# Turning x of the state-space part by DMA instead of on TensorE, in a two-block transformer kernel on one core

## The chip, the cores and the metric

The kernel runs on 1 core of one Trainium2 chip. The metric is the device time of one execution in microseconds (us), lower is better. The engines are PE (TensorE), DVE (VectorE), ACT (ScalarE), POOL (GpSimd) and SP (SyncE, which here only issues DMAs).

## The reference, cut to what matters

Two blocks of two layers each, on 256 tokens of width 1024, in float32. The change lies in the first block, in each of its two layers. There the input projection gives z, x, B, C, dt, q, k, v and gates. x, B and C go through a causal convolution of 4 taps and a silu; then x (2048 channels, 32 heads in 4 groups) runs through a chunked state-space scan:

```python
xbc = jax.nn.silu(causal_depthwise_conv(xbc, conv_w, conv_b)).astype(f32)
xs, bm, cm = jnp.split(xbc, [SSD_INNER, SSD_INNER + SSD_GROUPS * SSD_STATE], axis=-1)
x = (xh * dt[..., None]).reshape(bsz, nc, SSD_CHUNK, SSD_GROUPS, SSD_HPG, p)
y_diag = jnp.einsum("bgecls,bcsgep->bclgep", cb[:, :, None] * decay, x)
states = jnp.einsum("bclgn,bclgep->bcgepn", bc, x * decay_states[..., None])
y = ssd_chunked(xs, dt, a, bm, cm) + d_skip.astype(f32)[:, None] * xs
y = y.reshape(bsz, s, SSD_INNER) * jax.nn.silu(z.astype(f32))
yg = yg * lax.rsqrt(jnp.mean(yg * yg, axis=-1, keepdims=True) + RMS_EPS)
return (yg.reshape(bsz, s, SSD_INNER) * norm_w.astype(f32)).astype(z.dtype)
```

Beside it the layer has an attention with three query patterns over 8 heads (queries and keys are turned so that head channels lie on the partitions), and after it output projections and a gated feed-forward.

## The kernel before, in words

**The weight stream.** All large products run as three TensorE products on float32 values split in two: high times high, high times low, low times high. The weights come in chunks of 128 x 2048 (one `load` on SP into a ring of 3 slots, `w_raw`). ACT copies a chunk to `w_high` (`split_high`, L1180), DVE subtracts to `w_low` (`split_low`), PE multiplies (L676 to L678 with the tokens stationary, 24 products a chunk of 512 columns; L937 to L939, for x, B and C, with the weights stationary, 48 of 256). ACT's split of chunk c waits until PE has finished chunk c-3, SP's load of chunk c until DVE has split chunk c-3. Each engine's program is one loop over chunks c, and the small work is put between chunks by hand: "at c" below means in that engine's iteration c. ACT and DVE therefore reach their iteration c while PE is about at chunk c-2, and SP reaches its own while PE is about at c-5. Two chunks make a tile of 512 projected columns; x tiles are i = 2, 5, 8, 11 (`XT`), one for each group g.

**The state-space work of group g, before.** ACT convolves a part and takes the silu into `conv` at c = 2i+6. PE turns the eight 128 x 128 blocks of `conv` at c = 2i+5 into PSUM banks 4 and 5 (`turn`, L681; from group 1 on it first waits for `ssd_y`, the last sum of the group before, made by DVE). DVE reads the banks at c = 2i+7: `y` = x times d_skip, `xdt` = x times dt (two token tiles each), `xds`. PE at c = 2i+6 and 2i+8 spreads the rows of decays (L789, from `DR`, a small DMA `decay_rows`), at 2i+7 makes the new state from `xds` (L795), at 2i+9 and 2i+10 multiplies `xdt` by the masked decays `EM` (L802) and applies the state (L807). ACT takes exponentials of the spread rows (L1346), DVE masks them (L1949 and the next product).

**The small DMAs of SP.** The decay rows of group 0 are both loaded at SP's c = 13, those of the others at 2i+6 and 2i+8. Before the change SP issues at each c first the weight load, then a turn of q or k, then a turn of y, then one of attention weights, then decay rows.

**Turning by DMA.** y of each group, and seven of the eight query and key tiles, are turned by transfers: POOL lays the 16-bit halves of the float32 words apart (L1669 for y, L1662 for q and k), SP issues a transpose of 16-bit elements (L592, L581), and POOL (y, L1672) or ACT (q and k, L1325) puts the halves together. y then gets its norm weights on DVE, ACT copies it to `b_high`, DVE subtracts to `b_low`, all at c = 2i+16 (`Y_WEIGH`). POOL's program is one fixed order: for n = 0 to 3 the halves of q or k tile n, then those of y group n and their putting together.

**The last query tile** (`q5`) is turned by PE at c = 47 (`QK_LAST`) into banks 6 and 7. Bank 7 holds the output of attention head 3 until DVE has made its `b_low`, so PE waits for `o_ready` 4.

Of the kernel before, what the change touches and what calls it, by code (L numbers as in the profile page):

```python
# [143 lines left out]
def build(nc, stream, pars, const1, const2, onehot, relb, final_g, ple_g, w_x, out, rev):  # L144
    ctx = ExitStack()
    with ctx:
# [63 lines left out]
        def words(name, at_col, shape):  # L210
# [40 lines left out]
        y_back = [words("y_turned0", Q_AT + 1024, [2 * T * 512])[:, :], words("y_turned1", Q_AT + 1024, [2 * T * 512])[:, :],  # L251
                  early("y_turned2", 0, 20, 2 * T * 512, U16)[:, :], early("y_turned3", 0, 20, 2 * T * 512, U16)[:, :]]
        pT = E0[:, 1152:1536]
# [118 lines left out]
        xt_ps = signal("xt_ps", GROUPS)  # L372
# [5 lines left out]
        words_split = signal("words_split", 7 + GROUPS)  # L378
        words_turned = [signal("words_turned0", 16 * 6), signal("words_turned1", 16 * 5)]
# [34 lines left out]
        y_high = signal("y_high", 2 * GROUPS)  # L414
# [27 lines left out]
        xdt_ready = signal("xdt_ready", GROUPS)  # L442
# [3 lines left out]
        y_weighted = signal("y_weighted", 2 * GROUPS)  # L446
# [12 lines left out]
        xds_ready = signal("xds_ready", GROUPS)  # L459
# [100 lines left out]
        def _(sp):  # L560
# [14 lines left out]
            def turn_qk(l, c):  # L575

                for n, at_c in enumerate(QK_SPLIT):
                    m = QK_TURN[n]
                    if c == at_c + 3:
                        sp.wait_ge(words_split.sem, words_split.at(l, m + 1))  # L580
                        sp.dma_start_transpose(qk_turn[n].rearrange("p (m r) -> p m r", r=P), qk_half[n])\  # L581
                            .then_inc(words_turned[m % 2].sem, 16)

            def turn_y(l, c):

                for g, i in enumerate(XT):
                    m = Y_TURN[g]
                    if c == 2 * i + 16:
                        if g == 2:
                            sp.wait_ge(xt_ps.sem, xt_ps.at(l, GROUPS))  # L590
                        sp.wait_ge(words_split.sem, words_split.at(l, m + 1))
                        sp.dma_start_transpose(y_back[g].rearrange("p (m r) -> p m r", r=P), y_half[g])\  # L592
                            .then_inc(words_turned[m % 2].sem, 16)
# [80 lines left out]
        def _(pe):  # L674
# [42 lines left out]
            def before(l, c):  # L717
# [1684 lines left out]
```

## Time and profile before

| | |
|---|---|
| median of 3 runs | 1533.62 us (1533.17 to 1533.92) |
| the profiled execution: its time | 1532.54 us |
| its span (first to last instruction) | 1530.7 us |
| granted TensorE clock, mean | 0.999 |
| busy: PE, PE weight loads | 1510.8 us (99%), 1277.3 us (83%) |
| busy: DVE, ACT, POOL | 1043.2 us (68%), 919.3 us (60%), 178.5 us (12%) |
| DMA engines, mean busy share of the hardware queue | 58.3% |

The profile is of one execution. A busy time is the time in which an engine worked on an instruction; matmuls are pipelined, so that the distance from one start to the next tells what one costs, not its own length. The time of the profiled execution is 1.84 us above its span.

### The profile page before, as it was taken

How to read it: one execution, taken by the hardware profiler on the slowest of the kernel's cores; microseconds unless marked ns; L12 is line 12 of the kernel's file. 1: busy time of each engine (PE TensorE's matmuls, PEld its weight loads, DVE VectorE, ACT ScalarE, POOL GpSimd, SP SyncE). 2: the span in 40 equal slices, each digit the busy share in tenths (PEclk: the TensorE clock that was granted, in tenths of full speed). 3: DMA queues.
4: the chain of work that ended last, by engine and by line, in shares of the span. 5: the costliest groups of instructions: out<-in, count | busy, mean ns of one | idle time of the engine just before them, and what ended most of it. 6: DMA issues, size and time to landing. Idle time of an engine off the chain costs nothing.

```text
span 1530.7 us, 18991 instructions
## 1 busy us (share of the span) xinstructions
PE 1510.8 (99%) x7628; PEld 1277.3 (83%) x7628; DVE 1043.2 (68%) x1324; ACT 919.3 (60%) x1100; POOL 178.5 (12%) x113
## 2 busy tenths in 40 slices
PE   7999999999999999999999999999999999999998
PEld 7888888878888888988888888888888878888887
DVE  6978887856665555787887775666555576677665
ACT  5766786564355553667678565436555465666564
POOL 1001121412000100001112231100010020002000
PEclk9999999999999999999999999999999999999999
DMA  7456655766457775455556695547768574447541
GB/s 276 166 174 169 193 170 197 203 191 164 181 189 212 211 229 181 169 165 182 175 180 192 186 220 165 172 146 240 210 168 261 196 258 180 145 145 245 177 152 66
DMA packets 128239, 287.03 MB, mean 188 GB/s; under 512 B 92919, under 2 KB 93848, under 8 KB 97688
## 3 DMA queue, kind: packets, MB, share of 16 engines
q1 hardware_dynamic: 127048, 283.39, 58.3%
q10 hardware_dynamic: 1104, 2.43, 0.5%
q8 instruction: 60, 0.98, 0.2%
q14 instruction: 27, 0.22, 0.0%
HBM read 261.69 MB, written 1.84 MB: 172 GB/s over the span
## 4 chain that ended last, share of the span: by engine, by line
PE 86%; DVE 9%; ACT 3%; issue 1%; DMA 0%; ACTq 0%; DVEq 0%
PE ps L676 23%; PE ps L678 23%; PE ps L677 23%; DVE w_low L1706 3%; PE ps L681 3%; DVE conv L1792 2%; PE ps L937 2%; PE ps L939 2%; PE ps L938 2%; PE ps L824 1%; DVE scratch L1706 1%; ACT w_high L1180 1%; PE ps L802 1%; PE ps L826 1%; DVE xpad L1706 1%
## 5 line engine op out<-in xcount | busy, mean ns | idle before, releaser
L1706 DVE TENSOR_TENSOR w_low<-w_raw,w_high 128x2048 fp32r<-128x2048 f32 (+1 forms) x250 | 575.0, 2300 | 374.2 <-ACT w_high L1180 307.3
L676 PE MATMUL ps<-w_high,u_high 128*128 128x512 f32 x1376 | 547.8, 398 | 0.5 <-DVE w_low L1706 0.5
L678 PE MATMUL ps<-w_high,u_low 128*128 128x512 f32 x1376 | 537.0, 390 | 0.0
L677 PE MATMUL ps<-w_low,u_high 128*128 128x512 f32 x1376 | 536.2, 390 | 0.0
L1180 ACT ACTIVATE w_high<-w_raw 128x2048 fp32r<-128x2048 f32 (+1 forms) x196 | 369.1, 1883 | 250.5 <-PE ps L678 237.5
L676 PEld LDWEIGHTS ps<-w_high,u_high 128*128 128x128 f32 x1376 | 258.6, 188 | 55.2 <-issue 2.4
L678 PEld LDWEIGHTS ps<-w_high,u_low 128*128 128x128 f32 x1376 | 258.3, 188 | 55.1
L677 PEld LDWEIGHTS ps<-w_low,u_high 128*128 128x128 f32 x1376 | 258.8, 188 | 53.7 <-issue 2.4
L676 PE MATMUL ps<-w_high,b_high 128*128 128x512 f32 x384 | 151.6, 395 | 0.0
L678 PE MATMUL ps<-w_high,b_low 128*128 128x512 f32 x384 | 149.8, 390 | 0.0
L677 PE MATMUL ps<-w_low,b_high 128*128 128x512 f32 x384 | 149.6, 389 | 0.0
L1430 ACT ACTIVATE w_high<-w_raw 128x2048 fp32r<-128x2048 f32 x50 | 95.3, 1911 | 45.8 <-PE ps L678 45.6
L937 PE MATMUL ps<-u_high,w_high 128*128 128x256 f32 x384 | 112.8, 294 | 4.0 <-DVE w_low L1706 3.7
L938 PE MATMUL ps<-u_low,w_high 128*128 128x256 f32 x384 | 109.2, 284 | 0.0
L939 PE MATMUL ps<-u_high,w_low 128*128 128x256 f32 x384 | 109.2, 284 | 0.0
L1706 DVE TENSOR_TENSOR scratch<-scratch 128x128 f32<-128x128 f32 (+3 forms) x156 | 68.1, 470 | 34.5 <-ACT scratch L1373 27.1
L678 PEld LDWEIGHTS ps<-w_high,b_low 128*128 128x128 f32 x384 | 72.1, 188 | 15.2
L677 PEld LDWEIGHTS ps<-w_low,b_high 128*128 128x128 f32 x384 | 72.2, 188 | 14.5
L676 PEld LDWEIGHTS ps<-w_high,b_high 128*128 128x128 f32 x384 | 72.2, 188 | 14.2
L937 PEld LDWEIGHTS ps<-u_high,w_high 128*128 128x128 f32 x384 | 74.2, 193 | 6.5 <-DVE w_low L1706 4.1
L938 PEld LDWEIGHTS ps<-u_low,w_high 128*128 128x128 f32 x384 | 74.3, 194 | 1.7 <-issue 1.4
L939 PEld LDWEIGHTS ps<-u_high,w_low 128*128 128x128 f32 x384 | 74.2, 193 | 0.0
(242 smaller groups left out, 1512.3 us busy)
## 6 DMA issues: line engine op xcount, KB each, us to landing
w_raw<-in_stream SPq DMA_DIRECT2D x238, 1024.0 KB, 4.9
w_raw<-in_stream SPq DMA_DIRECT2D x12, 512.0 KB, 4.1
par<-in_pars SPq DMA_DIRECT2D x4, 269.0 KB, 5.7
h<-in_x SPq DMA_DIRECT2D x4, 256.0 KB, 4.9
ple_gain<-in_ple_g ACTq DMA_DIRECT2D x2, 512.0 KB, 4.8
out<-h SPq DMA_DIRECT2D x4, 256.0 KB, 2.0
scratch<-in_const SPq DMA_DIRECT2D x1, 768.0 KB, 7.3
rev<-scratch ACTq DMA_DIRECT2D x1, 768.0 KB, 3.6
```

Source lines behind the costliest of these rows:

```text
L676: nc.tensor.matmul(o, hi, whi, start=start, stop=False, **kw)
L677: nc.tensor.matmul(o, hi, wlo, start=False, stop=False, **kw)
L678: return nc.tensor.matmul(o, lo, whi, start=False, stop=stop, **kw)
L681: return nc.tensor.transpose(o, i, ident)
L802: last = nc.tensor.matmul(ps[:, 4 + t, e * HD:(e + 1) * HD], EM[t][:, e, :], xdt[:, t, e * HD:(e + 1) * HD], start=True, stop=True)
L937: nc.tensor.matmul(o, WH[:, slot, w], uH[:, kk, :], start=first, stop=False, skip_group_check=True)
L938: nc.tensor.matmul(o, WH[:, slot, w], uL[:, kk, :], start=False, stop=False, skip_group_check=True)
L939: last = nc.tensor.matmul(o, WL[:, slot, w], uH[:, kk, :], start=False, stop=kk == KD - 1, skip_group_check=True)
L1180: nc.scalar.activation(WH[:, c % RING, 0:n], W[:, c % RING, 0:n], ACT.Copy).then_inc(high_ready, 1)
L1430: nc.scalar.activation(WH[:, n % RING, :], W[:, n % RING, :], ACT.Copy).then_inc(high_ready, 1)
L1706: return nc.vector.tensor_tensor(out=o, in0=a, in1=b, op=op)
L1792: ins = nc.vector.scalar_tensor_tensor(out=conv[:, j, :], in0=xpad[:, j, k:k + S], scalar=par[:, w:w + 1], in1=conv[:, j, :], op0=ALU.mult ...
```

## The change

It does these things, in each of the two layers:

1. PE no longer turns `conv`. POOL lays the halves of `conv` apart (`split_x`, two copies), SP issues a transpose (`turn_x`, at c = 2i+9, ahead of all its other small DMAs of that c) into `x_turned`, which lies where `conv` lies, and POOL puts them together in `xdt` (`merge_x`).
2. DVE works from `xdt` at c = 2i+8 instead of from PSUM at 2i+7: y, `xds`, and then `xdt` times dt in place.
3. PE makes the new state at c = 2i+8, behind the decay rows of token tile 1, in bank 5; ACT copies it at 2i+10.
4. POOL's order becomes: x of group g, y of group g-1 (halves and putting together), then the halves of q or k tile g. y's transposes move from c = 2i+16 to 2i+17. The semaphores of the transfers go from two to three.
5. y's weighting is folded: ACT makes `b_high` by four scaled copies, DVE makes `b_low` by four fused multiply-subtracts (`Y_HIGH`, `Y_LOW`).
6. The last query tile is turned into banks 4 and 5, without the wait for `o_ready` 4. ACT's putting together of tile q2 moves from c = 30 to 31.

```diff
-        QK_TURN, Y_TURN = (0, 2, 4, 6, 8, 9, 10), (1, 3, 5, 7)
-        QK_MERGE = (14, 24, 30, 34, 46, 47, 48)
+        X_TURN, QK_TURN, Y_TURN = (0, 2, 5, 8), (1, 4, 7, 10, 12, 13, 14), (3, 6, 9, 11)
+        QK_MERGE = (14, 24, 31, 34, 46, 47, 48)
-        Y_WEIGH = 16
+        X_AT = 8
+        Y_HIGH, Y_LOW = (17, 17, 17, 16), (19, 19, 19, 16)
...
+            def turn_x(l, c):
+                for g, i in enumerate(XT):
+                    m = X_TURN[g]
+                    if c == 2 * i + 9:
+                        sp.wait_ge(words_split.sem, words_split.at(l, m + 1))
+                        sp.dma_start_transpose(x_back.rearrange("p (m r) -> p m r", r=P),
+                                               x_half.rearrange("p h t j n -> p (h t j n)")).then_inc(words_turned[m % 3].sem, 16)
...
-                    if c == 2 * i + 16:
+                    if c == 2 * i + 17:
...
+                    turn_x(l, c)
                     turn_qk(l, c)
                     turn_y(l, c)
...
-                    if c == 2 * i + 5:
-                        pe.wait_ge(conv_act.sem, conv_act.at(l, 3 + g))
-                        if g == 0:
-                            pe.wait_ge(btok_out.sem, btok_out.at(l, 1))
-                            pe.wait_ge(cumt_out.sem, cumt_out.at(l, 1))
-                        else:
-                            pe.wait_ge(ssd_y.sem, ssd_y.at(l, 2 * g))
-                        for t in range(T):
-                            for j in range(4):
-                                last = turn(ps[:, 4 + t, tok(j)], conv[:, j, tok(t)])
-                        last.then_inc(xt_ps.sem, 1)
...
-                    if c == 2 * i + 7:
-                        pe.wait_ge(xds_ready.sem, xds_ready.at(l, g + 1))
+                    if c == 2 * i + 8:
+                        pe.wait_ge(x_ready.sem, x_ready.at(l, 2 * g + 1))
...
-                        nc.tensor.matmul(ps[:, 6, :], btok[:, g, :], xds, start=True, stop=True).then_inc(state_ps.sem, 1)
+                        nc.tensor.matmul(ps[:, 5, :], btok[:, g, :], xds, start=True, stop=True).then_inc(state_ps.sem, 1)
...
                 if c == QK_LAST:
                     pe.wait_ge(roped.sem, roped.at(l, 8))
-                    pe.wait_ge(o_ready.sem, o_ready.at(l, 4))
...
+                        if c == 2 * i + Y_HIGH[g]:
+                            act.wait_ge(y_whole.sem, y_whole.at(l, g + 1))
+                            for j in range(4):
+                                jj = 4 * g + j
+                                ins = nc.scalar.activation(bH[:, jj, :].rearrange("p (t n) -> p t n", t=T), Y[g % 2][:, :, tok(j)],
+                                                           ACT.Identity, scale=par[:, C_SN + jj:C_SN + jj + 1])
...
+                def split_x(g):
+                    pool.wait_ge(conv_act.sem, conv_act.at(l, 3 + g))
+                    for t in range(T):
+                        ins = nc.gpsimd.tensor_copy(x_half[:, :, t], conv[:, :, tok(t)].bitcast(U16).rearrange("p j (n h) -> p h j n", h=2))
+                    ins.then_inc(words_split.sem, 1)
+
+                def merge_x(g):
+                    m = X_TURN[g]
+                    pool.wait_ge(words_turned[m % 3].sem, words_turned[m % 3].at(l, 16 * (m // 3 + 1)))
+                    if g:
+                        pool.wait_ge(yd_ps.sem, yd_ps.at(l, 2 * g))
+                    nc.gpsimd.tensor_copy(words_of(xdt).rearrange("p n h -> p h n"),
+                                          x_back.rearrange("p (h m) -> p h m", h=2)).then_inc(x_whole.sem, 1)
...
+                for g in range(GROUPS):
+                    split_x(g)
+                    if g == 0:
+                        split_qk(0)
+                    merge_x(g)
+                    if g:
+                        split_y(g - 1)
+                        merge_y(g - 1)
+                        split_qk(g)
+                split_y(3)
+                merge_y(3)
...
+                        if c == 2 * i + X_AT:
+                            dve.wait_ge(x_whole.sem, x_whole.at(l, g + 1))
...
+                            for t in range(T):
+                                tt(heads(y[:, t, :]), heads(xdt[:, t, :]),
+                                   bc(par[:, C_DS + g * HPG:C_DS + (g + 1) * HPG].unsqueeze(2), HPG, HD), ALU.mult)
+                            tt(heads(xds), heads(xdt[:, 0, :]), bc(dt_out[:, g * HPG:(g + 1) * HPG].unsqueeze(2), HPG, HD), ALU.mult)\
+                                .then_inc(x_ready.sem, 1)
```

## Rows read from the trace of the kernel before

**Rows 1.** The page's head and its busy time of PE.

```profile
span 1530.7 us, 18991 instructions
PE 1510.8 (99%) x7628; PEld 1277.3 (83%) x7628; DVE 1043.2 (68%) x1324; ACT 919.3 (60%) x1100; POOL 178.5 (12%) x113
```

**Rows 2.** Who waited for whom: us in total, times, longest us.

```profile
ACT w_high L1180 <- PE ps L678: 237.5, 109, 4.5
...
PE ps L681 <- DVE b_low L1706: 3.4, 2, 1.7
```

**Rows 3.** Instructions on `conv`, and what ended the idle time before them.

```profile
L681 PE MATMUL ps<-con,conv x64: 270/273/301, 70.6 to 793.6; 128*128 128x128 f32 x64
...
  DVE scratch L1706: 1.6, 4
```

**Rows 4.** PE's timeline in group 0: start us, us, engine, line, what.

```profile
70.27 0.39 PE L678 MATMUL ps<-w_high,u_low 128*128 128x512 f32 x1
70.59 1.06 PE L681 MATMUL ps<-con,conv 128*128 128x128 f32 x8
...
71.72 0.39 PE L677 MATMUL ps<-w_low,u_high 128*128 128x512 f32 x1
...
76.96 0.63 PE L789 MATMUL ps<-decay_rows,steps_r 128*128 128x512 f32 x2
...
89.78 0.63 PE L789 MATMUL ps<-decay_rows,steps_r 128*128 128x512 f32 x2
```

**Rows 5.** PE's timeline where the last query tile is turned.

```profile
319.89 0.39 PE L678 MATMUL ps<-w_high,u_low 128*128 128x512 f32 x1
321.98 1.06 PE L681 MATMUL ps<-con,scratch 128*128 128x128 f32 x8 [1.71 <-DVE b_low L1706]
```

**Rows 6.** ACT's timeline: the silu of x, group 0.

```profile
67.62 1.06 ACT L1272 ACTIVATE conv<-conv 128x1024 f32<-128x1024 f32 x1 [3.39 <-DVE conv L1792]
```

**Rows 7.** DVE's timeline: two stretches of group 0, one later.

```profile
67.50 2.29 DVE L1706 TENSOR_TENSOR w_low<-w_raw,w_high 128x2048 fp32r<-128x2048 f32 x1
...
83.91 1.21 DVE L1706 TENSOR_TENSOR ssd_decay<-ssd_decay,scratch 128x1016 f32<-128x1016 f32 x1
...
246.32 3.95 DVE L1706 TENSOR_TENSOR w_low<-w_raw,w_high 128x2048 fp32r<-128x2048 f32 x1 [2.87 <-ACT w_high L1180]
```

**Rows 8.** POOL's timeline: laying halves apart, and putting y together.

```profile
79.75 1.89 POOL L1662 COPY qk_halves<-scratch 128x2048 uint16<-128x2048 uint16 x1 [49.52 <-DVE scratch L1706]
...
245.67 2.51 POOL L1672 COPY scratch<-y_turned 128x2048 uint16<-128x2048 uint16 x1 [4.36 <-DMA y_turned<-y_halves]
```

**Rows 9.** POOL's groups by form: count, then busy us and mean ns.

```profile
L1682 POOL COPY act_halves<-scratch 128x1024 uint16<-128x1024 uint16 x22 | 22.9, 1041 | 338.3 <-DVE scratch L1706 338.3
```

**Rows 10.** SP's timeline of issues: start us, us that SP was held.

```profile
69.81 0.33 SPq L606 DMA_DIRECT2D w_raw<-in_stream  x1
70.26 1.53 SPq L573 DMA_DIRECT2D decay_rows<-cum_rows  x2
...
84.32 5.28 SPq L581 DMA_TRANSPOSE qk_turned<-qk_halves  x1
...
119.23 3.16 SPq L592 DMA_TRANSPOSE y_turned<-y_halves  x1
```

**Rows 11.** DMA issues: count, KB each where told, median us from issue to landing.

```profile
w_raw<-in_stream SPq DMA_DIRECT2D x238, 1024.0 KB, 4.9
...
qk_turned<-qk_halves SPq DMA_TRANSPOSE x14, 7.4
...
y_turned<-y_halves SPq DMA_TRANSPOSE x8, 4.3
```

**Rows 12.** DVE's groups by form: count, then busy us and mean ns.

```profile
L1792 DVE SCALAR_TENSOR_TENSOR conv<-xpad,par,conv 128x256 f32<-128x256 f32 x144 | 60.1, 480 | 0.9
...
L1706 DVE TENSOR_TENSOR scratch<-ps,par 128x512 f32<-128x512 f32 x32 | 21.7, 684 | 7.9 <-PE ps L681 7.9
...
L1706 DVE TENSOR_TENSOR scratch<-scratch,par 128x512 f32<-128x512 f32 x16 | 13.7, 895 | 0.0
```

More of the change, by code:

```diff
@@ L377, in build @@
         qk_ps = signal("qk_ps", 1)
-        words_split = signal("words_split", 7 + GROUPS)
-        words_turned = [signal("words_turned0", 16 * 6), signal("words_turned1", 16 * 5)]
+        words_split = signal("words_split", 7 + 2 * GROUPS)
+        words_turned = [signal(f"words_turned{i}", 16 * 5) for i in range(3)]
+        x_whole = signal("x_whole", GROUPS)
         y_whole = signal("y_whole", GROUPS)
@@ L809, in before @@
                     pe.wait_ge(roped.sem, roped.at(l, 8))
-                    pe.wait_ge(o_ready.sem, o_ready.at(l, 4))
                     for hh in range(4):
                         for t in range(T):
-                            last = turn(ps[:, 6 + hh // 2, (hh % 2) * S + t * P:(hh % 2) * S + (t + 1) * P], ev[QK[7][2]][:, t, tok(hh)])
+                            last = turn(ps[:, 4 + hh // 2, (hh % 2) * S + t * P:(hh % 2) * S + (t + 1) * P], ev[QK[7][2]][:, t, tok(hh)])
                     last.then_inc(qk_ps.sem, 1)
@@ L1348, in _ @@
                                 ins.then_inc(ssd_exp.sem, 1)
+                        if c == 2 * i + 10:
+                            act.wait_ge(state_ps.sem, state_ps.at(l, g + 1))
+                            if g:
+                                act.wait_ge(off_ps.sem, off_ps.at(l, g))
+                            nc.scalar.activation(state, ps[:, 5, :], ACT.Copy).then_inc(state_out.sem, 1)
                         if c == 2 * i + 13:
@@ L1359, in _ @@
                             nc.scalar.activation(gsum, gsum, ACT.Sqrt, bias=eps1, scale=GROUPS / INNER).then_inc(group_root.sem, 1)
-                        if c == 2 * i + Y_WEIGH:
-                            for t in range(T):
-                                act.wait_ge(y_weighted.sem, y_weighted.at(l, 2 * g + t + 1))
-                                nc.scalar.activation(bH[:, 4 * g:4 * g + 4, tok(t)], four(Y[g % 2][:, t, :]), ACT.Copy)\
-                                    .then_inc(y_high.sem, 1)
+                        if c == 2 * i + Y_HIGH[g]:
[4 more added lines that the diff above has]
+                                                           ACT.Identity, scale=par[:, C_SN + jj:C_SN + jj + 1])
+                            ins.then_inc(y_high.sem, 1)
                     for n in range(8):
@@ L1951, in _ @@
                                     .then_inc(ssd_m.sem, 1)
+                        if c == 2 * i + X_AT:
+                            dve.wait_ge(x_whole.sem, x_whole.at(l, g + 1))
+                            if g >= 2:
+                                dve.wait_ge(y_ready.sem, y_ready.at(l, 2 * g - 2))
+                            if g:
+                                dve.wait_ge(state_ps.sem, state_ps.at(l, g))
+                            else:
+                                dve.wait_ge(decays.sem, decays.at(l, 1))
+                                chain.then(dve, tt(dt_out, dt[:, 0:HEADS], dec_out, ALU.mult))
+                            for t in range(T):
[3 more added lines that the diff above has]
+                                .then_inc(x_ready.sem, 1)
+                            for t in range(T):
+                                ins = tt(heads(xdt[:, t, :]), heads(xdt[:, t, :]),
+                                         bc(dt[:, t * HEADS + g * HPG:t * HEADS + (g + 1) * HPG].unsqueeze(2), HPG, HD), ALU.mult)
+                            ins.then_inc(x_ready.sem, 1)
                         if c == 2 * i + 12:
@@ L1973, in _ @@
                             convolve(l, n, c - 2 * i - CONV_AT)
+                    for g, i in enumerate(XT):
+                        if c == 2 * i + Y_LOW[g]:
+                            dve.wait_ge(y_high.sem, y_high.at(l, g + 1))
+                            for j in range(4):
+                                jj = 4 * g + j
+                                ins = nc.vector.scalar_tensor_tensor(
+                                    out=bL[:, jj, :].rearrange("p (t n) -> p t n", t=T), in0=Y[g % 2][:, :, tok(j)],
+                                    scalar=par[:, C_SN + jj:C_SN + jj + 1],
+                                    in1=bH[:, jj, :].bitcast(F32).rearrange("p (t n) -> p t n", t=T), op0=ALU.mult, op1=ALU.subtract)
+                            ins.then_inc(y_ready.sem, 2)
                     for n, (name, i, e, _) in enumerate(QK):
```

113 lines of the change are left out of this document (48 added, 65 removed).

## The prediction

> **What bounds the kernel now.** I read the page's head first: PE is busy 99% of the span [rows 1]. On this page that alone doesn't say that PE is the bound, since overlapping matmuls count as busy, so I looked at who waits for whom. ACT, which prepares the weights, stands idle for 237.5 us until PE has freed a slot, and PE's largest wait for another engine inside a layer is one of 3.4 us in two pieces [rows 2]. So the weight stream runs ahead of PE, and PE's own instruction stream sets the time. What a change is worth is then what it takes out of PE's stream, less every wait that it puts in. The reader should look at PE's timeline around one insert: products, eight small ones, products again without a pause [rows 4].
>
> **The sum is made for the profiled execution**, 1532.54 us (span 1530.7 and 1.84 around it). The median of the runs shown is 1533.62, so 1.08 is added at the end.
>
> **What leaves PE.** (a) The turns of conv, 64 matmuls in 8 blocks [rows 3]. In group 0 the last product before the block starts at 70.27, the second one after it at 71.72, 1.45 us later. From 71.72 to the next insert at 76.96 there are 23 steps, 0.228 us each [rows 4]. Two steps would have taken 0.46, so a block costs 0.99 us and eight cost 7.9. (b) PE's waits for ssd_y right before these blocks, 1.6 us in 4 places [rows 3]. The insert that asks for ssd_y next comes one chunk later (some 5.5 us, the distance of 24 steps), far more than the 0.4 of each wait, so they don't come back. (c) The last query tile: the product before it starts at 319.89, the turn at 321.98, and the wait for b_low of head 3 is named there with 1.71 [rows 5], in total 3.4 for both layers [rows 2]. Banks 4 and 5 are free by then, because the scores of head 3 were read before the rope of that tile, in DVE's order. What is late next is the scores of head 4, which wait for ACT's copy of the turned tile; ACT makes it behind the split of chunk 49, and PE has a whole chunk of products before it asks. I take 3.4. Sum of what leaves: 12.9 us.
>
> **What moves on PE** is the state product. It now follows directly on the spreading of decays, an insert that is there anyway. The number of instructions is the same. I cost it at nothing, from -0.2 to +0.2 a group.
>
> **What comes in: the decay rows of group 0.** SP issues both of them at c = 13, and turn_x of group 0 is at c = 13 too and stands ahead. This is the one place where a new transfer is on PE's path. Step by step, on the clock of the trace of before:
> - The silu of x ends at 67.62 + 1.06 = 68.68 [rows 6]. POOL then makes two copies of 1024 words each; the same size costs 1.04 [rows 9]. DVE has begun a w_low at 67.50 that takes 2.29 [rows 7], and if POOL must wait for it, the copies run from 69.79 to 71.87; if not, they end at 70.8.
> - SP has issued its weight load at 69.81 and then issued the rows from 70.26 at once [rows 10]. Now it waits until 71.87, and the transpose holds it: 3.16 us for y's with nothing ahead, 5.28 for a q or k one behind a weight load [rows 10]. So SP comes free between 75.0 and 77.1, and the rows of token tile 0 need half of 1.53 more.
> - A transpose lands 4.3 us after its issue (y, mostly alone) or 7.4 (q and k, behind a load) [rows 11]: at 76.2 or at 79.3. The weight load ahead of it is 2.1 us old of its 4.9 [rows 11], so 2.8 us of it are left, which the 3.16 that SP needs in any case mostly cover. I take 1.3 us above the lower end: 77.5 for transpose and rows behind it.
> - PE comes to L789 at 76.96 - 0.99 = 75.97 [rows 4]. It waits 1.5 us. The bounds are 0 (rows land as soon as they are issued, 75.8) and 3.3 (behind a transpose that takes 7.4).
>
> Two layers: 3.0 us, from 0 to 6.6. No other group has this, since their rows are issued at 2i+6 and 2i+8 and turn_x at 2i+9.
>
> The Trainium skill (DMA: Bandwidth & Descriptors, section on queues, rings and completion order) says that a DMA engine takes the descriptors of a ring in order and that a completion is only written after the engine's earlier writes. By it the rows can't be reported before the transpose, so the wait is at least 76.2 - 75.97 = 0.2 us; no row of this trace shows a small transfer behind a transpose.
>
> **The rest, costed at nothing, with its cover.** Chain of x in group 0: POOL does the halves of k0 before merge_x. Even where they stand now, at 79.75 for 1.89, the merge (2.51, as y's [rows 8]) would end at 84.2; DVE wants xdt when its mask of the decays ends, 83.91 + 1.21 = 85.1 [rows 7]. Three products follow (0.68 each [rows 12]), and PE asks for xds behind L789 at 89.78 + 0.5 [rows 4]: 87.1 against 90.3, some 3 us of cover, less about 1 in later groups, where PE has gained on it. The weight loads behind a transpose on SP start up to 5.3 us late (ring of three, one chunk of 5.5 us each). DVE gets lighter: y loses two products of 0.895 and two subtracts, and gets four fused ones of 0.48 [rows 12]. ACT gets four scaled copies for two plain ones, under 1 us a group, against 237.5 us of waiting for PE [rows 2].
>
> **Result of the sum:** 12.9 - 3.0 = 9.9 us; 1522.6 for the profiled execution, 1523.7 for the median.
>
> **Rivals.**
> - A, the rows come in time (POOL's copies don't wait for DVE and the small transfer is quick): nothing is paid, 12.9 us gained, 1520.7. For it: 70.8 + 3.16 + 0.8 = 74.8, before 75.97. Against it: the load in front. 0.16.
> - B, slower: DVE and POOL hold each other. A w_low that began 0.65 us after POOL's merge of y took 3.95 instead of 2.29, and would have begun its work when that merge ended at 248.18 [rows 7, 8]. Per group three new POOL copies come, and they fall where DVE splits chunk 2i+8 and works on x. If the merge of x and the halves of y hold it back to back, 2.51 + 1.89 = 4.4 us, the 2 to 3 us of cover are gone and PE waits for xds some 2.2 us in each of 8 groups: 17.6 - 9.9 = 7.7 us slower, 1541.3. It decides from 1.2 us of wait a group on. Against it: merge_x waits for its transfer, and by the numbers above the merge of group 0 is over before DVE's mask is. 0.08. The Trainium skill (SBUF — State Buffer, section on the two separate sides) says that a DVE instruction with two inputs in SBUF and a GpSimd one exclude each other for their whole length, and an input in PSUM is no part of this. The trace agrees with the first (3.95); by the rule the products on x, which read PSUM before and don't now, join those that can be held.
> - C, the last group's y: its transpose moves one c on and behind a weight load (7.4 in place of 4.3), while its b_high stays at c = 38, ahead of the exponentials and weight splits on ACT. If PE then waits in the first attention heads, up to 2.5 us a layer, 5 of the 9.9 go: 1528.7. For it: it is the only y stage without its extra chunk. Against it: two chunks of stream lie ahead. 0.13.
> - D, nothing is gained (within 0.2%): the stream of weights falls back by as much as PE gains, and PE waits for w_low. Against it stands the 237.5 us [rows 2]. 0.06.
>
> **Chances and range.** The likeliest case, the sum with its rows of group 0 late, 0.57; its own range is 1520.7 to 1527.3 (0 to 6.6 us paid). A measurement of this kernel tells 0.2%, 3.07 us, from no change. Faster by more: 0.57 + 0.16 + 0.13 = 0.86. Same: D, 0.06. Slower: B, 0.08. The range reaches from A with a little more at the turned query tile (1.86 by the starts of rows 5 in place of 1.71), 1520.0, over C to 1529.5; B and D stay outside.
>
> **What would show it.** PE has no L681 on conv and no wait for b_low or ssd_y. A new wait of 1 to 2 us at L789, once a layer, ended by a DMA of decay_rows. SP's timeline has a DMA_TRANSPOSE of 3 to 5.3 us right before the two rows of group 0. If PE waits at L795 for a DVE product, B is at work; if it waits at L824 or for w_low about chunks 38 to 42, C or D. The prediction is wrong if the rows of group 0 wait much over 3.3 us, or if waits for x appear in all groups.

## The result, and the profile after

The changed kernel takes 1545.51 us (1544.63 to 1548.32) beside 1533.53 for the kernel before on the same chip: a ratio of 1.0082, 95% interval [1.0068, 1.0096]. It is 0.8% slower. The prediction of 1523.7 (1520.0 to 1529.5), with 0.86 for faster, was wrong. The profiled execution took 1545.49 us.

The page's head, beside [rows 1]:

```profile
span 1543.2 us, 18921 instructions
...
PE 1511.1 (98%) x7564; PEld 1275.6 (83%) x7564; DVE 1064.4 (69%) x1324; ACT 924.0 (60%) x1116; POOL 254.8 (17%) x137
```

PE has 64 instructions fewer, as meant, yet is as busy as before (1511.1 against 1510.8), although the prediction had put the turns at 7.9 us. And the span is 12.5 us longer. So two things need finding: time in which PE waits, and time in which it works slower.

What PE waits for (total, times, longest), beside [rows 2]:

```profile
PE ps L799 <- DVE scratch L1749: 14.2, 4, 5.0
...
PE ps L789 <- DMA decay_rows<-cum_rows: 2.8, 2, 1.4
```

The waits for `b_low` (3.4) and `ssd_y` (1.6) are gone. In their place stands L799, the state product, which waits for DVE's `xds` in 4 places: in groups 2 and 3 of each layer. PE's timeline in group 2 of the first layer:

```profile
168.90 0.63 PE L789 MATMUL ps<-decay_rows,steps_r 128*128 128x512 f32 x2
172.53 1.13 PE L799 MATMUL ps<-scratch 128*128 128x512 f32 x2 [2.99 <-DVE scratch L1749]
```

What DVE did in these microseconds (its timeline; compare [rows 7]):

```profile
159.77 1.66 DVE L2014 SCALAR_TENSOR_TENSOR b_low<-scratch,par,b_high 128x256 fp32r<-128x256 f32 x4
164.06 3.71 DVE L1749 TENSOR_TENSOR w_low<-w_raw,w_high 128x2048 fp32r<-128x2048 f32 x1 [2.62 <-ACT w_high L1186]
167.69 1.86 DVE L1975 COPY ssd_decay<-scratch 128x8 f32<-128x8 f32 x1
169.46 1.21 DVE L1749 TENSOR_TENSOR ssd_decay<-ssd_decay,scratch 128x1016 f32<-128x1016 f32 x1
170.59 1.28 DVE L1749 TENSOR_TENSOR scratch<-xdt,par 128x512 f32<-128x512 f32 x2
171.79 0.68 DVE L1749 TENSOR_TENSOR scratch<-xdt,small 128x512 f32<-128x512 f32 x1
```

and POOL's timeline beside it:

```profile
163.12 2.56 POOL L1670 COPY xdt<-x_turned 128x2048 uint16<-128x2048 uint16 x1 [10.65 <-DMA x_turned<-x_halves]
165.60 3.92 POOL L1678 COPY y_halves<-scratch 128x2048 uint16<-128x2048 uint16 x1
```

Read them together. DVE's `w_low` starts at 164.06, while POOL's merge of x runs until 165.68, and takes 3.71 where one alone takes 2.29 [rows 7]. POOL's next copy, the halves of y, starts at 165.60 and is itself held by `w_low`; when `w_low` ends at 167.77, the halves hold DVE's next instruction, a copy of 128 x 8 elements, until 169.52. It takes 1.86. DVE lost 1.42 + 1.69 = 3.1 us, and PE's gap is 2.99. DVE never waits for `x_whole`: the transfer of x is in time, but it is in time at the wrong moment.

The same two instructions are held for 2.6, 2.6 and 3.0 us in the other three places (`w_low` takes 3.16, 3.16 and 3.63 there, the small copy 1.86 each time), 11.3 us in all, beside 14.2 us of waits.

Why the merge stands there is seen on SP's timeline (start, time that SP was held; compare [rows 10]):

```profile
154.64 0.34 SPq L616 DMA_DIRECT2D w_raw<-in_stream  x1
155.03 5.48 SPq L591 DMA_TRANSPOSE x_turned<-x_halves  x1
```

POOL has the halves of x ready at 152.47. SP issues a weight load at 154.64 first, and the transpose behind it holds SP for 5.48 us and lands at 163.07.

The slower work shows when stretches are asked for (columns: us, then busy us and count of PE, PEld, DVE, ACT, POOL; then the granted clock, DMA share, GB/s):

```profile
217.00:221.80 4.80, 4.80 (x10) 3.09 (x11) 4.77 (x10) 4.09 (x5) 2.66 (x1) 0.50 0.55 108
778.30:781.60 3.30, 3.30 (x9) 2.61 (x8) 3.30 (x8) 1.10 (x2) 2.00 (x1) 0.50 0.25 55
822.70:826.00 3.30, 3.30 (x9) 2.20 (x8) 3.30 (x6) 3.21 (x5) 1.55 (x1) 0.50 0.41 92
1242.50:1245.80 3.30, 3.30 (x9) 2.61 (x8) 0.62 (x1) 3.30 (x5) 0.00 (x0) 0.50 0.91 313
222.00:228.00 6.00, 6.00 (x36) 5.26 (x35) 6.00 (x5) 2.10 (x2) 5.35 (x2) 1.00 0.54 198
```

In four stretches the granted clock is 0.50, that is 1.2 in place of 2.4 GHz. The starts of the stream's products lie 0.43 us apart there, where [rows 4] give 0.228:

```profile
1239.11 2.84 PE L1046 MATMUL ps<-scratch 33*128 33x384 f32 x8
...
1243.29 0.63 PE L688 MATMUL ps<-w_low,u_high 128*128 128x512 f32 x1
1243.72 0.63 PE L689 MATMUL ps<-w_high,u_low 128*128 128x512 f32 x1
```

The stretches run from 215.04 to 221.87 (PE stands until 216.80 of it), and over 3.41 us each from 778.24, 822.61 and 1242.45. PE works 5.07 + 3 x 3.41 = 15.3 us in them; at half speed that is 7.6 us lost, an estimate (with 0.228 in place of 0.43 a step it would be 7.1). Before, only the tail after 1528.9 was at that clock. The first three begin during or right behind PE's waits at L799 of 4.98, 2.41 and 3.83 us; ahead of the fourth PE has no gap over 0.3 us, but the block of eight small products shown above (33 rows each, 1239.11 to 1241.95).

The balance: 12.9 us leave by the prediction's sum, 2.8 + 14.2 + 7.6 = 24.6 come, 11.7 more in all; the spans of the two profiled executions differ by 12.5 and their times by 12.95.

The place of group 0 that the prediction had priced, PE's timeline and SP's:

```profile
75.87 0.39 PE L689 MATMUL ps<-w_high,u_low 128*128 128x512 f32 x1
77.64 0.71 PE L789 MATMUL ps<-decay_rows,steps_r 128*128 128x512 f32 x2 [1.39 <-DMA decay_rows<-cum_rows]
```

```profile
71.84 3.42 SPq L591 DMA_TRANSPOSE x_turned<-x_halves  x1
75.39 1.53 SPq L574 DMA_DIRECT2D decay_rows<-cum_rows  x2
```

### The profile page after: what moved, and what is told of

Its sections match the earlier page's. It is cut to its first block, busy times and chain, and to the rows that moved or that the text cites. A ratio compares the mean times of both kernels' runs of the same rounds, so it can differ in the third digit from the quotient of the medians.

```text
span 1543.2 us, 18921 instructions
## 1 busy us (share of the span) xinstructions
PE 1511.1 (98%) x7564; PEld 1275.6 (83%) x7564; DVE 1064.4 (69%) x1324; ACT 924.0 (60%) x1116; POOL 254.8 (17%) x137
## 4 chain that ended last, share of the span: by engine, by line
PE 79%; DVE 13%; ACT 4%; issue 3%; DMA 0%; SPq 0%; POOL 0%; ACTq 0%; DVEq 0%
PE ps L687 22%; PE ps L689 22%; PE ps L688 22%; DVE w_low L1749 4%; DVE conv L1835 3%; DVE scratch L1749 2%; PE ps L692 2%; PE ps L943 2%; PE ps L944 1%; PE ps L945 1%; PE ps L830 1%; ACT w_high L1186 1%; PE ps L808 1%; DVE ssd_decay L1975 1%; ACT ssd_decay L1349 1%
## 5 line engine op out<-in xcount | busy, mean ns | idle before, releaser
L1749 DVE TENSOR_TENSOR scratch<-scratch 128x128 f32<-128x128 f32 (+3 forms) x156 | 83.3, 566 | 34.6 <-ACT scratch L1383 27.2
L689 PEld LDWEIGHTS ps<-w_high,b_low 128*128 128x128 f32 x384 | 72.1, 188 | 15.3
L1725 POOL COPY act_halves<-scratch 128x1024 uint16<-128x1024 uint16 x22 | 22.9, 1043 | 340.1 <-DVE scratch L1749 340.1
```

The source lines that it names most:

```text
L689: return nc.tensor.matmul(o, lo, whi, start=False, stop=stop, **kw)
L1725: nc.gpsimd.tensor_copy(act_half[j % 2][:, :].rearrange("p (h n) -> p h n", h=2), ac_words[j % 2].rearrange("p n h -> p h n")).then_inc(ac ...
L1749: return nc.vector.tensor_tensor(out=o, in0=a, in1=b, op=op)
```

## The experiments

The theories. **Hold** (rival B of the prediction): DVE and POOL exclude each other; the merge of x and the halves of y fall on DVE's `w_low` and small copy and make `xds` late. **Place**: PE now asks for `xds` at a point where DVE can't have it, whatever holds it, since two products of y and the mask stand ahead in DVE's order. **Cascade**: wherever the state product stands, the lateness comes back at the next thing that depends on it. The kernel before ran beside each, with medians of 1533.1 to 1533.6; ratios are against it.

### 1. POOL: halves of y ahead of the merge of x

```diff
-                    merge_x(g)
                     if g:
                         split_y(g - 1)
+                    merge_x(g)
+                    if g:
                         merge_y(g - 1)
```

> The changed kernel with POOL's order altered in one place: the halves of y of group g-1 are laid apart before x of group g is put together, not after it. All copies and all waits for data stay. Theory hold (DVE and POOL exclude each other, and two POOL copies back to back hold DVE's w_low and then the small copy ahead of the mask, so xds comes late): POOL then does y's halves while x is still under way, only one copy falls on chunk 2i+8, the small copy isn't held for 1.7 us, and PE's waits for xds fall from 14.2 us to 5 or less, TensorE's clock stays at its upper level in most places, 1531 to 1536. Theory place (PE asks for the state one chunk too early, whatever POOL does): the waits stay over 10 us, 1541 to 1546.

Measured: 1532.68 us, ratio 1.0000 [0.9991, 1.0009]; 12.8 us less than the changed kernel, from swapping two copies of POOL. L799 waits 6.8 us in place of 14.2 (hold had said 5 or less), no stretch before the tail is at the lower clock, and PE is busy 1503.8 us, 7.3 less. DVE's timeline at the same place, and POOL's:

```profile
164.63 3.52 DVE L1750 TENSOR_TENSOR w_low<-w_raw,w_high 128x2048 fp32r<-128x2048 f32 x1 [0.98 <-ACT w_high L1186]
168.07 0.16 DVE L1976 COPY ssd_decay<-scratch 128x8 f32<-128x8 f32 x1
```

```profile
160.50 2.08 POOL L1678 COPY y_halves<-scratch 128x2048 uint16<-128x2048 uint16 x1 [7.44 <-DVE scratch L2005]
163.46 2.59 POOL L1670 COPY xdt<-x_turned 128x2048 uint16<-128x2048 uint16 x1 [0.88 <-DMA x_turned<-x_halves]
```

The small copy is back at 0.16, since the halves of y are over before `w_low` starts; `w_low` is still held by the merge (3.52). Place is refuted as the main cause: PE asks where it asked, DVE's order is what it was. It isn't excluded for a part of the 6.8 us that are left.

### 2. The state product a chunk later

PE's product first, ACT's copy of the state second:

```diff
-                    if c == 2 * i + 8:
+                    if c == 2 * i + 9:
-                        if c == 2 * i + 10:
+                        if c == 2 * i + 11:
```

> The changed kernel with PE's state product at 2i+9 and ACT's copy of it at 2i+11, one chunk later each; POOL and DVE unaltered. Hold and place both expect that the waits for xds go (14.2 us) and with them the time that PE spent at the lower clock behind them (some 7 us): 1523 to 1526. A third theory, cascade (DVE has fallen behind the weight stream, and what isn't waited for here is waited for at the next w_low or decay product), expects new waits at the products with decays or at w_low and 1533 or more.

Measured: 1545.41 us, 1.0080 [1.0065, 1.0095]: nothing gained, where hold and place had said 1523 to 1526. L799 has no wait any more, but another has come up:

```profile
PE ps L808 <- ACT scratch L1356: 11.4, 4, 3.4
```

PE's product with the state waits for ACT's copy of it. On ACT that copy stands behind the convolution of the next part, which waited 5.25 us for DVE's `xpad`, and `b_high`:

```profile
185.83 2.08 ACT L1272 ACTIVATE conv<-xpad,par 128x256 f32<-128x256 f32 x4 [5.25 <-DVE xpad L1749]
187.81 1.69 ACT L1372 ACTIVATE b_high<-scratch,par 128x256 fp32r<-128x256 f32 x4
189.41 0.57 ACT L1356 ACTIVATE scratch<-ps 128x512 f32<-128x512 f32 x1
```

Giving PE's instruction a chunk more time gave the wait to the next one. And the lower clock stayed: four stretches behind or at these waits, in which PE works 19.1 us, about 9.5 us lost by the same estimate (7.6 in the changed kernel). Cascade holds for this edit.

### 3. The kernel before with the last query tile in banks 4 and 5

```diff
-                    pe.wait_ge(o_ready.sem, o_ready.at(l, 4))
-                            last = turn(ps[:, 6 + hh // 2, ...
+                            last = turn(ps[:, 4 + hh // 2, ...
```

> The kernel before with one part of the change alone: the last query tile is turned into banks 4 and 5 without the wait for head 3's low part. The prediction's step says 3.4 us less than before (3.7 by the starts of the products): 1530.0 +- 0.3, the wait for b_low gone. The rival for this step is that the wait turns up again at the scores of head 4, then 1533.5.

Measured: 1529.57 us, 0.9975 [0.9965, 0.9984]: 0.25% of 1533 is 3.8 us, against a term of 3.4, a little more than was expected. The wait for `b_low` is gone and nothing took its place.

### 4. The products on x ahead of the second mask

DVE's block of products on x at 2i+8 is moved as a whole ahead of its mask of the decays at the same c.

> The changed kernel with DVE's products on x ahead of the mask of the decays within chunk 2i+8; POOL and PE unaltered. Hold: the small copy that was held for 1.7 us and the mask of 1.2 us no longer stand ahead of xds, which comes some 3 us earlier, so PE's waits of 3.0, 5.0, 2.4 and 3.8 us shrink to about 0, 2, 0 and 1: 1529 to 1534. Place: DVE is simply too full between the split of 2i+8 and PE's question, the mask comes late in its stead and PE waits at the product with decays, 1540 or more.

Measured: 1543.81 us, 1.0071 [1.0054, 1.0088]. L799 waits 12.4 us in 4 places. This missed what the hold theory said (1529 to 1534), and the time is what place had said (1540 or more), but not for place's reason: no wait came up at the products with decays. The holds moved: in group 2 `w_low` began first and POOL's merge of x was held to 4.13 us; DVE waited 2.44 us for it, and then the halves of y held the two products of y, which took 2.92 us in place of 1.28. Reordering DVE without moving POOL's copies only changes who is held.

### 5. Halves of y first, and the rows ahead of the transpose

```diff
+                    for t in range(T):
+                        if c == 13:
+                            load_rows(l, 0, t)
                     turn_x(l, c)
```

> Two edits together: the halves of y ahead of the merge of x (1532.68 by itself), and the two decay rows of group 0 issued ahead of turn_x at c = 13. The rows' waits at L789 were 2.8 us in the changed kernel and 2.9 with the first edit. Theory that the two costs are separate: the sum, 1532.7 - 2.9 = 1529.8, and no wait of PE at L789 for decay_rows; the x of group 0 lands 1.5 us later and has the cover. Rival, the late transpose costs what the rows gain: PE waits at L799 in group 0 too, and the time stays at 1532 to 1533.

Measured: 1532.06 us (1527.86 to 1535.29), 0.9990 [0.9981, 0.9999]. The waits at L789's place are gone and L799's stay at 6.9. The median moved by 0.6 us where 2.9 were expected; its executions lie 7.4 us apart, and the spread goes with the clock: the mean granted clock is 0.995 in the slowest and 0.999 in the fastest. The two profiled executions can be laid side by side by the starts of the same products of the weight stream. The two places of the rows are 3.4 us shorter than in experiment 1; against that stand 1.6 us for a stretch of 3.41 us at the lower clock, from 1226.89, that experiment 1 doesn't have, and 0.6 us within the first 20 us. That leaves 1.2, and they differ by 1.2 (1530.93 and 1529.70). So the rows' gain is there, and the clock took half of it.

### 6. The same, and turn_x ahead of the weight load

```diff
+                    if c != 13:
+                        turn_x(l, c)
                     if l or c > 1:
                         load(l * CHUNKS1 + c, c % RING, l * BLOCKS1 + c, 0, CH)
```

> The kernel of the last run, and for groups 1 to 3 turn_x stands ahead of SP's weight load of the same c. In the run with the halves first the load was issued at 155.23 and the transpose held SP from 155.61 to 160.84 and landed at 163.41, so that POOL's merge of x (163.46 to 166.06) still meets w_low (164.63 to 168.15, 3.52 us in place of 2.29). Theory hold: the transpose is now issued at 155.2 with nothing ahead, lands about 160, the merge follows the halves of y at 162.6 and ends near w_low's start; w_low takes 2.3 to 2.9, and most of the 6.8 us of waits at L799 go: 1524 to 1527. Rival, the weight load that starts 3 to 5 us late makes DVE and ACT late: no gain or a loss, 1530 to 1534, with ACT and DVE waiting for w_raw.

Measured: 1529.94 us, 0.9977 [0.9967, 0.9987]; L799's waits are still 6.2 us in 4 places, and three stretches of 3.41 us are at the lower clock in the profiled execution (1531.42). This missed what hold had said (1524 to 1527), and it isn't the rival either: ACT and DVE don't wait for `w_raw`. The transfer lands early, but POOL, which now makes the halves of y first, gets to the merge only when y is there, and holds `b_low` instead of `w_low`. POOL's timeline and DVE's:

```profile
158.15 2.09 POOL L1684 COPY y_halves<-scratch 128x2048 uint16<-128x2048 uint16 x1 [7.44 <-DVE scratch L2011]
160.18 2.75 POOL L1676 COPY xdt<-x_turned 128x2048 uint16<-128x2048 uint16 x1
```

```profile
158.40 5.14 DVE L2021 SCALAR_TENSOR_TENSOR b_low<-scratch,par,b_high 128x256 fp32r<-128x256 f32 x3
163.46 2.28 DVE L1756 TENSOR_TENSOR w_low<-w_raw,w_high 128x2048 fp32r<-128x2048 f32 x1
```

### 7. The changed kernel with turn_x ahead of the load, nothing else

> The changed kernel with one edit on SP alone: turn_x of groups 1 to 3 ahead of the weight load of the same c. POOL's order is untouched (merge of x, then halves of y). Theory hold: the merge runs about 160 to 162.6 in group 2 and the halves of y 162.6 to 164.6, so both are over when w_low starts at 164; w_low(24) falls from 3.71 to 2.3 to 2.6, the small copy L1975 from 1.86 to 0.17, the 14.2 us at L799 fall under 7 and the stretches at a granted clock of 0.5 go: 1531 to 1536. Theory place (PE asks at a place where DVE's products can't be ready, whatever holds them): L799 keeps 10 us or more, 1541 or more. Theory late loads: ACT waits for w_raw, 1545 or more.

Measured: 1526.44 us, 0.9957 [0.9945, 0.9970]: 19 us faster than the changed kernel, 0.4% faster than before and 5 us better than hold had given, from the order of two issues on SP in three iterations of each layer. SP's, POOL's and DVE's timelines in group 2:

```profile
153.19 1.96 SPq L591 DMA_TRANSPOSE x_turned<-x_halves  x1
```

```profile
157.50 3.54 POOL L1673 COPY xdt<-x_turned 128x2048 uint16<-128x2048 uint16 x1 [4.33 <-DMA x_turned<-x_halves]
161.77 2.09 POOL L1681 COPY y_halves<-scratch 128x2048 uint16<-128x2048 uint16 x1 [0.73 <-DVE scratch L2007]
```

```profile
156.37 2.28 DVE L1752 TENSOR_TENSOR w_low<-w_raw,w_high 128x2048 fp32r<-128x2048 f32 x1
159.66 2.05 DVE L2007 TENSOR_SCALAR scratch<-scratch,small 128x512 f32<-128x512 f32 x2
161.63 3.30 DVE L2017 SCALAR_TENSOR_TENSOR b_low<-scratch,par,b_high 128x256 fp32r<-128x256 f32 x4
164.85 2.28 DVE L1752 TENSOR_TENSOR w_low<-w_raw,w_high 128x2048 fp32r<-128x2048 f32 x1
167.05 0.17 DVE L1978 COPY ssd_decay<-scratch 128x8 f32<-128x8 f32 x1
```

The transpose with nothing ahead holds SP for 1.96 us and lands at 157.44, 5.6 us earlier. Holds remain (L2007 takes 2.05 in place of 0.88, `b_low` 3.30 in place of 1.66), but they fall into the 2.62 us in which DVE had waited for ACT's `w_high`; that wait is gone from the row of `w_low`. From there on DVE runs free. L799's waits (L802 here) are 1.8 us in 2 places, and only the tail is at the lower clock: 12.4 + 7.6 = 20.0 us less, measured 19.05 between the profiled executions. Late loads don't show, and of place no more than these 1.8 us could.

### 8. Experiment 5 and the state product a chunk later

> The kernel with the halves of y first and the rows ahead, and PE's state product at 2i+9 with ACT's copy at 2i+11. Moved alone, the wait came back behind ACT's copy: 11.4 us at L808. Theory hold: with DVE no longer held the remaining lag is 1 to 2 us a place; PE has a chunk of 5.5 us before it asks for xds, but ACT's copy again stands behind the conv work that waits for DVE, so a part returns at L808: 2 to 6 us there in place of 6.8 at L799, 1526 to 1530. Theory cascade (the move costs by itself, whatever DVE does): L808 keeps about 11 us, 1535 or more.

Measured: 1537.91 us, 1.0030 [1.0018, 1.0042], 5.9 slower than experiment 5. L811 waits 9.8 us for ACT's copy in 4 places. The profiled execution, 1540.66, has PE at the lower clock for 20.5 us, in five stretches. Even with DVE less held the move costs by itself: this went as cascade said, by more than hold allowed.

### 9. Experiment 7 and the rows ahead

> The kernel with turn_x of groups 1 to 3 ahead of SP's weight load (1526.44) and, besides, the two decay rows of group 0 issued ahead of turn_x at c = 13. Its waits at L792 for decay_rows are 2.8 us. Theory that these are a cost of their own: they go and nothing comes for them, 1523.6, the time that was predicted for the changed kernel. Rival: x of group 0 comes 1.5 us later and PE waits at L799's place in group 0, 1526 to 1527.

Measured: 1526.25 us (1523.46 to 1529.73), 0.9949 [0.9936, 0.9962]. The rows' waits (2.8) are gone; the state product waits 3.8 us in 3 places in place of 1.8 in 2, with 2.6 in group 3 of the first layer. By the medians nothing is left of the 2.8. Laid beside experiment 7's profiled execution, product by product, this one is 3.3 us shorter at the two places of the rows, 1.7 longer at that wait, and 1.6 longer in a stretch of 3.41 us at the lower clock, from 1223.51, that experiment 7 doesn't have. The executions whose mean granted clock is 1.000 lie at 1523.46 and 1523.63 here and at 1525.80, 1526.44 and 1526.66 in experiment 7: 2.7 us apart, what the rows were to give, in few executions.

### 10. The kernel before with y's weights folded

ACT's and DVE's blocks of part 5 in the kernel before, at c = 2i+17 and 2i+18 (last group 16).

> The kernel before with part 5 alone: the norm weights of y folded into ACT's four scaled copies (c = 2i+17, last group 16) and DVE's four fused multiply-subtracts (2i+18, last group 16). The prediction costed it at nothing, since ACT and DVE wait for PE: 1532.5 to 1534. Rival: the fused products, two inputs in SBUF like the ones they replace but 3.3 us long in one row in the run with the halves first, hold POOL or are held by it and make DVE late: waits of PE for b_low or ssd_y grow, 1535 or more.

Measured: 1531.19 us, 0.9985 [0.9976, 0.9994], 2.4 us faster, where nothing was expected. The waits of PE for `ssd_y` ahead of the turns (1.6 us, [rows 3]) are gone in it, and each of the four places is 0.59 us shorter by the starts of the products around it, 2.4 in all. The prediction had put this gain to the account of the insert that is gone; folding alone brings it too. Whether it does so because DVE has less to do (1035.7 us busy in place of 1043.2) or because it does it one and two iterations later wasn't separated. The fused product alone takes 0.48 in this kernel, as taken.

### 11. The changed kernel with half of the merge of x

```diff
-                    nc.gpsimd.tensor_copy(words_of(xdt)..., x_back...)
+                    n = 512 if g else 1024
+                    nc.gpsimd.tensor_copy(words_of(xdt)...[:, :, 0:n], x_back...[:, :, 0:n])
```

> The changed kernel, but in groups 1 to 3 POOL puts together only the words of token tile 0 (1024 elements of 16 bits in place of 2048); this leaves out x of token tile 1 in these groups. Everything else, the transfers and the orders, is as in the changed kernel. Theory hold: POOL's merge takes some 1.3 us in place of 2.56, DVE's w_low beside it is held 1.2 us less (2.5 in place of 3.71), the halves of y follow earlier, and L799 waits 1 us less in each of 4 places, 9 to 11 us in total in place of 14.2, with part of the low clock gone: 1536 to 1542. Theory place, and any in which POOL's length doesn't matter: L799 at 13 us or more, 1544 or more.

This kernel leaves out half of x in groups 1 to 3 and serves for its time alone. Measured: 1538.91 us, 1.0033 [1.0022, 1.0043], inside what hold gave. In group 2 POOL's copy takes 1.38 us, `w_low` 2.40; L799 waits 11.2 us, and 9.9 us of PE's work are at the lower clock in place of 15.3. The waits fell by 3.0 and the clock's loss by 2.7; the profiled executions differ by 5.7. The small copy still takes 1.86, held by the halves of y, whose copy takes 3.93; in two of the other three places the halves, now earlier, hold `w_low` instead (3.85 and 3.80). Nothing but the length of one copy of POOL was changed, and DVE never waits for what it makes: this is the hold, measured by itself.

### 12. Experiment 9 and xds ahead of the products of y

```diff
+                            tt(heads(xds), ...).then_inc(x_ready.sem, 1)
                             for t in range(T):
                                 tt(heads(y[:, t, :]), heads(xdt[:, t, :]), ...)
-                            tt(heads(xds), ...).then_inc(x_ready.sem, 1)
```

> The kernel with turn_x ahead of the load and the rows ahead (1526.25), and DVE makes xds before the two products of y instead of after them. PE asks for xds alone at this place; the two products take 1.28 us together in the rows, so xds comes 1.28 us earlier. The waits left at L805 are 3.8 us in 3 places, the longest 2.6, in group 3 of the first layer. Theory hold, with DVE's lateness small by now: they fall by 1.28 each to some 1.3 us in one place, 1523 to 1525. Rival: what is left at that place isn't made of DVE's order but of its lag behind POOL, which the change moves only within a group; the wait stays over 3 us, 1526 or more.

Measured: 1521.60 us (1519.92 to 1522.14), 0.9919 [0.9906, 0.9933]: the fastest of all, 0.8% faster than before, 24 us faster than the changed kernel and below what hold had given (1523 to 1525). Against experiment 9's profiled execution it is 3.6 us shorter in the waits at the state product and 1.6 in the stretch at the lower clock, which isn't there; they differ by 5.2. What is left at the state product:

```profile
PE ps L805 <- DVE scratch L1755: 0.2, 1, 0.2
```

## Why the prediction was wrong, by its own steps

**What leaves PE: 12.9 us, right in sum.** In the traces of the kernel before and of experiment 12, the same products of the weight stream start 0.80 to 0.90 us closer together around each of the eight blocks of turns, 6.6 us in place of the 7.9 that were taken; 0.58 more in each of the four places with a wait for `ssd_y`, 2.3 in place of 1.6; and 1.90 and 1.89 at the last query tile, 3.8 in place of 3.4, as in experiment 3. That is 12.7 us. The move of the state product costs nothing, as taken (0.86 less at the old place, 0.85 more at the new one). The profiled executions differ by only 10.9, because 1.4 us of the difference were lost in the first 20 us: there PE's products of 256 columns follow each other every 0.21 us until 13.4 in the kernel before and until 15.9 in experiment 12, and every 0.12 us after. The waits for `ssd_y` also go by the folding of y's weights, without any change to x (experiment 10); whether the prediction's reason, that the next insert comes a chunk later, is enough without the folding wasn't run.

**The decay rows of group 0: right.** 1.5 us a layer were taken, 1.39 and 1.42 measured. SP was held 3.42 us, and the transpose landed at 77.14, where 77.5 stood. The Trainium skill (DMA: Bandwidth & Descriptors, section on queues, rings and completion order) says that a DMA engine writes a completion only after its own earlier writes, from which the prediction worked out that the rows can't be reported before the transpose ahead of them. PE's L789 starts at 77.64, after 77.14, which agrees.

**The step that failed is the chain of x, in "The rest, costed at nothing, with its cover".** It was wrong in two terms.

First, the 3 us of cover were worked out in group 0, with the merge of x as the only thing that could be late. What came late was not x, but DVE itself: held 3.1 us in group 2 by two copies of POOL, on `w_low` and on a copy of 128 x 8 elements that the sum didn't name at all. The merge of x is new, and the halves of y are an old copy that now stands right behind it.

Second, the cover was carried to the later groups "less about 1". In the changed kernel `xds` was ready 2.25 us before PE asked in group 0; in group 2 it came 3.1 us late, which is what DVE was held there, so that without the hold nothing would have been left of the cover. What shows in the rows is the start of `w_low`, each time right behind ACT's `w_high`: 7.8 us before PE asks in group 0, 7.6 in group 1, 5.3 in group 2 and 2.8 in group 3 of the first layer, while the chain from there to `xds` takes 5.3 to 5.5 unheld. So every microsecond of hold became one of waiting in groups 2 and 3. In group 3 the wait is 4.98 and the hold 2.6; the rest was brought along from before. How much of that goes back to earlier holds (at 176.86 and 181.61 DVE's rows are 2.1 and 1.7 longer than alone) and why `w_high` comes so late isn't shown. Experiment 7, in which neither instruction is held, has 0.2 and 1.0 us of lateness left in these groups.

In group 1 only `w_low` is held, by the halves of y, and PE doesn't wait:

```profile
122.22 3.99 DVE L1749 TENSOR_TENSOR w_low<-w_raw,w_high 128x2048 fp32r<-128x2048 f32 x1 [4.21 <-ACT w_high L1186]
126.14 0.16 DVE L1975 COPY ssd_decay<-scratch 128x8 f32<-128x8 f32 x1
```

In groups 2 and 3 the halves of y hold the small copy as well. POOL's three copies a group became six; I priced them by their own length and not by whom they hold.

**Rival B was the case**, at 0.08. It named the mechanism, the two copies back to back, and a time of 1541.3 (2.2 us in 8 places, 17.6 in all). Measured are 14.2 in 4 places. What it lacked is the clock: 7.6 us. That its 1541.3 lies near 1545.5 is partly luck: half the places, each longer, and a term that wasn't in it. Its counter-argument, that the merge is over before DVE's mask ends, was true (165.68 against 170.66) and beside the point, since the merge then lay on the `w_low` ahead of the mask. The Trainium skill (SBUF — State Buffer, section on the two separate sides) says that a DVE instruction in a two-port mode is as exclusive against GpSimd as one with two inputs in SBUF; the prediction used only the second half. The trace agrees as far as it goes: the small copy, with one input, took 1.86 beside the halves of y and 0.16 without; no row tells in which mode it runs.

**The transfer behind a weight load** stood in the prediction (3.16 us against 5.28, landing after 4.3 or 7.4) and was used for group 0 and the last y alone. For x of the later groups it decides all: experiment 7 moves this one issue and takes back 19 us.

**A, C and D** did not occur. PE has no wait at the last group's y, and none for the weight stream that it didn't have before.

**Still open.** What starts the stretch at the lower clock near 1223 to 1243, which the profiles of five of the kernels have (the changed one, experiments 5, 6, 8, 9) and the others not, without a wait of PE ahead of it. It is also what hides the rows' 2.8 us in experiments 5 and 9. In all five it begins between 0.1 us before and 0.7 us after the end of the block of eight products of 33 rows shown above. But the same block stands in every kernel here, in the others without such a stretch, so the block alone doesn't explain it.

## What to carry to other kernels

A copy on POOL is not priced by its length but by the DVE instructions that it meets: lay the two timelines side by side at every place where it will run, not only at the first, and look for the moment at which DVE waits anyway. That moment is set by the transfer that feeds the copy, so the order of two issues on a queue (a transpose ahead of a large load, not behind) can be worth more than the work that the change saves. The cover has to be read at every such place too: here it was 2.25 us in one group and nothing in another. Moving the instruction that waits a stage later does not help where the next consumer is as close; making its input first on the engine that is late does.

## What the runs showed of the hardware

- A wait of PE can cost more than its length. Three of the four waits at L799 (2.4 to 5.0 us) were accompanied by stretches at a granted clock of 0.50 (1.2 GHz), with 0.43 us from one product to the next in place of 0.23: some 7.6 us, one stretch without a wait included, beside 14.2 us of waiting. The wait of 2.99 us at 172.53 had no such stretch, while in experiment 2 one of 1.67 us, ending at 145.19, was followed by one from 146.23. The stretch at 1242.45 had no wait.
- A DMA transpose of the same size held SP for 1.96 us with nothing ahead of it (experiment 7), 3.42 behind a load that was 1.9 us old (the changed kernel, 71.84), and 5.2 to 5.5 right behind one. The median from issue to landing of x went from 7.2 to 4.3 us when six of its eight issues stood ahead of the load (that of y went from 6.4 to 7.5):

```profile
x_turned<-x_halves SPq DMA_TRANSPOSE x8, 7.2
```

```profile
x_turned<-x_halves SPq DMA_TRANSPOSE x8, 4.3
```

- The smallest DVE instruction can be held for many times its own length. In the changed kernel 10 of 16 copies of 128 x 8 elements took 1.86 us or more, before 3 of 16. The mean of the 128 x 8 copy, of which 0.17 is its own length, was 611 ns before and 1305 ns in the changed kernel (DVE's groups by form: count, then busy us and mean ns):

```profile
L1949 DVE COPY ssd_decay<-scratch 128x8 f32<-128x8 f32 x16 | 9.8, 611 | 0.0
```

```profile
L1975 DVE COPY ssd_decay<-scratch 128x8 f32<-128x8 f32 x16 | 20.9, 1305 | 0.0
```
